# Interleaving the stages of neighbouring tiles on TensorE, with a ring of five x blocks and eleven weight slots

## The reference

```python
h = rmsnorm(x, norm_mix);  proj = h @ w_in            # 1024 -> 2048: u | gb | gc | v, 512 channels each
d = trailing_means(u, windows 2/4/8/16) - u           # along time, per group of 128 channels
a = (d @ w_pool[group]) * pool_scale
b = gb * causal_dwconv3(gc * v)
x = x + concat(a, b) @ w_out                          # 1024 -> 1024
h = rmsnorm(x, norm_ffn);  up = h @ w_up              # 1024 -> 5632
upc = causal_dwconv3(up) + bias;  val, gate = split(upc)
x = x + (silu(gate) * val) @ w_down                   # 2816 -> 1024
y = rmsnorm(x, norm_final)
```

## Time and profile before

| | |
|---|---|
| median of 3 runs | 826.86 us |
| the profiled execution | 826.7 us, its slowest core (1) spans 825.2 us |
| other cores | 806.0 to 824.5 us |
| mean granted TensorE clock, core 1 | 0.979 |
| PE busy | 722.6 us, 88% |
| DVE, ACT, POOL busy | 504.9, 358.9, 194.9 us |
| weight units | 120, of 512 KB as they land, 6.9 us from issue to landing |
| chain that ended last | PE 57%, DMA 14%, DVE 11%, ACT 8%, issue 7% |

### The profile page before, as it was taken

The page is one execution under the profiler, slowest core; times in us unless marked ns, Lnnn a source line. Parts: engine busy times, 40 slices in busy tenths (PEclk is TensorE's granted clock), DMA queues, the critical chain, the costliest instruction groups (busy, mean ns, idle before and its releaser), DMA issues.

```text
span 825.2 us, 12962 instructions; the slowest of 8 cores (806.0 to 825.2 us)
## 1 busy us (share of the span) xinstructions
PE 722.6 (88%) x3826; PEld 337.1 (41%) x3826; DVE 504.9 (61%) x878; ACT 358.9 (43%) x846; POOL 194.9 (24%) x381
## 2 busy tenths in 40 slices
PE   0296788889999998999999879999999898999996
PEld 0143344344445433444444334444444334444442
DVE  0446477668864466677753475677743576788822
ACT  1223337556662233365652333466642332666621
POOL 3022005444530010044420010144420010244300
PEclk9998899999999999999999999999999899999999
DMA  8959727976642198179962394199842591499421
GB/s 204 217 85 150 124 33 110 170 124 106 116 86 78 65 195 187 26 128 148 148 114 100 103 213 95 26 154 155 151 81 99 166 172 21 81 152 154 84 91 68
DMA packets 27751, 98.69 MB, mean 120 GB/s; under 512 B 3470, under 2 KB 3982, under 8 KB 27682
## 3 DMA queue, kind: packets, MB, share of 16 engines
q0 software_dynamic: 19584, 70.92, 51.9%
q1 hardware_dynamic: 8098, 26.95, 9.8%
HBM read 158.75 MB, written 10.01 MB: 205 GB/s over the span
## 4 chain that ended last, share of the span: by engine, by line
PE 57%; DMA 14%; DVE 11%; ACT 8%; issue 7%; SPq 1%; DVEq 0%; POOL 0%; ACTq 0%; POOLq 0%
PE G L446 39%; DMA wslot<-w_str 9%; PE G L660 8%; PE G L661 8%; DMA x<-xp 3%; ACT hbuf L387 3%; DMA xrot<-xp 2%; DVE x L669 1%; DVE x L668 1%; ACT arena L770 1%; PE TR L410 1%; ACT hb L387 1%; ACT rs_all L389 1%; PE G L686 1%; DVE hbuf L399 1%
## 5 line engine op out<-in xcount | busy, mean ns | idle before, releaser
L446 PE MATMUL G<-aT,wslot 128*128 128x512 bf16 x1408 | 311.8, 381 | 5.7 <-ACT Esave L795 2.3
L446 PEld LDWEIGHTS G<-aT,wslot 128*128 128x128 bf16 x1408 | 136.4, 98 | 172.1 <-issue 15.6
L770 ACT ACTIVATE arena<-G,cst_sb 128x512 f32<-128x512 f32 x176 | 134.3, 774 | 102.0 <-PE G L446 102.0
L779 DVE SCALAR_TENSOR_TENSOR arena<-G,cst_sb,arena 128x512 f32<-128x512 f32 x176 | 130.0, 748 | 58.6 <-ACT Esave L795 37.4
L446 PE MATMUL G<-hT,wslot 128*128 128x512 bf16 x512 | 121.6, 396 | 27.3 <-DVE hT L414 8.1
L364 POOL DMA_DIRECT2D wslot<-w_str x120 | 68.6, 572 | 322.4 <-PE G L446 286.3
L660 PE MATMUL G<-w_down_sb,actT 128*128 128x512 bf16 x352 | 133.4, 379 | 1.0 <-POOL actT L799 1.0
L661 PE MATMUL G<-w_down_sb,actT 128*128 128x512 bf16 x352 | 133.4, 379 | 0.0
L799 POOL TENSOR_TENSOR actT<-arena 128x512 bf16<-128x512 f32 x88 | 95.5, 1085 | 149.8 <-ACT arena L766 84.4
L788 DVE SCALAR_TENSOR_TENSOR arena<-G,cst_sb,arena 128x512 f32<-128x512 f32 x176 | 125.5, 744 | 4.9 <-DVE OFp L786 0.5
L387 ACT ACTIVATE hbuf<-x 128x1024 bf16<-128x1024 f32 x34 | 35.9, 1057 | 123.9 <-DVE x L669 119.0
(11 more groups left out here) (115 smaller groups left out, 585.8 us busy)
## 6 DMA issues: line engine op xcount, KB each, us to landing
wslot<-w_str POOLq DMA_DIRECT2D x120, 512.0 KB, 6.9
x<-xp SPq DMA_DIRECT2D x16, 512.0 KB, 13.6
yp<-x SPq DMA_DIRECT2D x16, 512.0 KB, 2.8
xrot<-xp SPq DMA_DIRECT2D x12, 512.0 KB, 12.5
w_down_sb<-w_down POOLq DMA_DIRECT2D x11, 512.0 KB, 13.0
w_out_sb<-w_out POOLq DMA_DIRECT2D x4, 512.0 KB, 20.3
stf_sb<-st_ffn SPq DMA_DIRECT2D x1, 704.0 KB, 9.8
o_ffn_s<-stf_sb SPq DMA_DIRECT2D x1, 704.0 KB, 3.7
```

Source lines behind the costliest of these rows:

```text
L446: ins = e.matmul(out_ap, lhsT=wslot[slot][:, k, half * 128:(half + 1) * 128], rhs=rhsT[:, k, 0:ncols], start=(k == 0), stop=(k == nk - 1))
L770: P.op("act", lambda e, tp=tp, g=g, c=c, h=h: e.activation(out=tp[:, h, 2:514], in_=G[g][:, :], func=AF.Identity, scale=cc(C_FW + 3 * c), ...
L779: P.op("dve", lambda e, tp=tp, g=g, c=c, h=h: e.scalar_tensor_tensor(out=tp[:, h, 1:513], in0=G[g][:, :], scalar=cc(C_FW + 3 * c + 1), in1 ...
```

## The change

- **Order on PE.** Behind stage 3 of tile s comes stage 1 of tile s+1 at once, then a new function `window`: blocks 0 to 2 of stage 4 of tile s, the four stage 2 blocks of tile s+1, and block 3 of stage 4 of tile s in three parts (k 0 to 8, 9 to 16, 17 to 21) with the last transposes of stage 2 between them. The stage 0 blocks of tile s+2 are woven into the stage 4 blocks; the fourth stands behind the first stage 2 block. Stage 0 of tile 1 is woven into stage 2 of tile 0.
- **x blocks.** `x1` becomes a ring of `NX` = 5 blocks. The block (s+1, i+1) is loaded by `load_x1` behind the store of block (s, i), into the place which that store frees.
- **Weights.** The small tile's buffers move into one area `sm_arena` of 8 blocks. Once they are dead (in the window of tile 0) seven of the blocks become weight slots 4 to 10, and the eighth the fifth x block. A unit is now issued when a slot is released (`release`, `pump`), and the w_down pieces are spread over the units up to the 30th.
- **Loads at the start.** SP loads the four x blocks first, then constants, small x and states; st_ffn and gfin wait for stage 1. POOL issues four weight units ahead of its constants. The first stage 1 pair runs block by block.
- **Smaller edits.** No warm matmuls. Stage 1's last pool matmuls (`laters`) run behind the first five k of two stage 2 blocks (tile 0), or behind the first stage 4 block. In tile 0 the small tile's stage 2 follows the four blocks, and its stage 3 matmuls run one step ahead. In stage 3 the history copy follows the two evictions.

```diff
 NW = 4
-DEBUG = False
-WARM_S2, WARM_S3A, WARM_S3B, WARM_S1 = 6, 12, 6, 6
+NX = 5
...
+        def xr_of(s, i):
+            return (4 * s + i) % NX
+
+        def load_x1(s, i):
+            r = xr_of(s, i)
+            r0 = (s * 4 + i) * 128
...
+            P.op("sp", lambda e: e.dma_start(out=x1[r], in_=xp[r0:r0 + 128, :]),
+                 writes=[("x1", r)] + extra, dsem=f"D_x1_{r}")
...
+        def norm1_block(s, i):
+            if s == 0:
+                src, sk = x1[i], ("x1", i)
+            else:
+                b = 4 * s + i
+                src, sk = xrot[b % 2][:], ("xrot", b % 2)
+                r0 = b * 128
+                P.op("sp", lambda e: e.dma_start(out=src, in_=xp[r0:r0 + 128, :]), writes=[sk], dsem=f"D_xrot{b % 2}")
+            hb, hk = next_hb()
+            return hb_done(hk, norm_transpose(src, 128, [sk], hb, hk, hT, i * 128, C_G1, [("hT", i)]))
...
+        def window(s, laters):
+            nx2 = s + 2 if s + 2 < NST else None
+
+            def n1(i):
+                return norm1_block(nx2, i) if nx2 is not None else (lambda: None)
+            load_x1(s + 1, 0)
+            pb = n1(0)
+            for i in range(3):
+                post = s4_block(s, i)
+                if i == 0:
+                    for fn in laters:
+                        fn()
+                pb()
+                post()
+                if i + 1 < 4:
+                    load_x1(s + 1, i + 1)
+                pb = n1(i + 1)
+            if s == 0:
+                s4_small()
+                free_slots.extend(range(NW, NW + 7))
+                pump()
+            n2 = []
             for i in range(4):
...
+                n2.append(s2_block(s + 1, i))
+                if i == 0:
                     pb()
...
+                if i >= 2:
+                    n2.pop(0)()
+            gab = (galloc(), galloc())
+            s4_mm(3, ALLK[0:9], True, False, gab)
+            n2.pop(0)()
+            s4_mm(3, ALLK[9:17], False, False, gab)
+            n2.pop(0)()
+            s4_mm(3, ALLK[17:NFF], False, True, gab)
+            return lambda: s4_post(s, 3, gab)
```

More of the change, by code:

```diff
@@ L207, in psum @@
             return es.enter_context(nc.psum_tensor(name, shape, dt))
-        wslot = [sb(f"wslot{i}", [128, 8, 256], BF16) for i in range(NW)]
+        wslot = [sb(f"wslot{i}", [128, 8, 256], BF16)[:] for i in range(NW)]
         w_out_sb = sb("w_out_sb", [128, 8, D], BF16)
@@ new lines, in build_nc, with pump @@
+        assert [i for k, i in plan if k == "r"] == list(range(len(resident)))
+        plan.reverse()
+        free_slots = list(range(NW))
+        slot_of = {}
+        alias_done = set()
+        def pump():
+            while plan:
+                kind, i = plan[-1]
+                if kind == "r":
+                    plan.pop()
+                    dst, src, key, name = resident[i]
+                    P.op("pool", lambda e, dst=dst, src=src: e.dma_start(out=dst, in_=src), writes=[key], dsem=name)
+                    continue
+                if not free_slots:
+                    return
+                plan.pop()
+                slot = free_slots.pop(0)
+                slot_of[i] = slot
+                extra = []
+                if slot >= NW and slot not in alias_done:
+                    alias_done.add(slot)
+                    extra = alias_keys[slot]
+                t = wplan[i]
+                P.op("pool", lambda e, slot=slot, t=t: e.dma_start(
+                    out=wslot[slot].rearrange("p a b -> p (a b)"), in_=w_str[t, :, :]),
+                    writes=[("W", slot)] + extra, dsem=f"D_w{slot}")
@@ new lines, in f, with s2_mm @@
+                for n, k in enumerate(ks):
+                    st, sp = first and n == 0, last and n == len(ks) - 1
+                    e.matmul(G[ga][0:nrows, :], lhsT=lhsT_of_k(k), rhs=wsb[:, k, 0:512], start=st, stop=sp)
+                    ins = e.matmul(G[gb][0:nrows, :], lhsT=lhsT_of_k(k), rhs=wsb[:, k, 512:1024], start=st, stop=sp)
+                return ins
+            P.op("pe", f, reads=[lkey_of_k(k) for k in ks] + list(wkeys), writes=[gk(ga), gk(gb), gt(ga), gt(gb)])
+        def s2_mm(i, ks, first, last, gab):
+            mm_part(lambda k: aT[:, k, i * 128:(i + 1) * 128], lambda k: ("aT", k, i), 128, w_out_sb, WOUT_KEYS,
+                    ks, first, last, *gab)
@@ L939, in build_nc @@
-        while res_i[0] < len(resident):
-            issue_resident(1)
+        pump()
+        mk_ident()
+        P.op("pool", mk_consts, writes=["epst", "invcnt", "zeros"])
+        load_states_s1()
+        pbs = []
+        for i in range(4):
+            pbs.append(norm1_block(0, i))
+            if i >= 1:
+                pbs.pop(0)()
+        pbs.pop(0)()
+        norm_transpose(xs_sb[0:NSM, :], NSM, ["xs"], hs, "hs", hTs, 0, C_G1, ["hTs"])()
+        laters = stage1(0)
+        load_states_s3()
@@ new lines, in build_nc @@
+        gabs = {}
+        for i in range(2):
+            gabs[i] = (galloc(), galloc())
+            s2_mm(i, S2_KORDER[0:5], True, False, gabs[i])
+        for fn in laters:
+            fn()
+        n2 = []
+        pb = norm1_block(1, 0)
+        for i in range(4):
+            if i < 2:
+                s2_mm(i, S2_KORDER[5:], False, True, gabs[i])
+                n2.append(s2_post(0, i, gabs[i]))
+            else:
+                n2.append(s2_block(0, i))
+            pb()
+            if i >= 1:
+                n2.pop(0)()
+            if i < 3:
+                pb = norm1_block(1, i + 1)
@@ new lines, in build_nc @@
+        sm2 = s2_small()
+        for fn in n2:
+            fn()
+        for s in range(NST):
+            last = (s == NST - 1)
+            if s == 0:
+                stage3(0, sm2)
+                sample_state_outputs()
+            else:
+                stage3(s)
+            if last:
+                prompt_state_outputs()
+                gabs = [(galloc(), galloc()) for _ in range(2)]
+                for i in range(2):
+                    s4_mm(i, ALLK[0:NFF - 1], True, False, gabs[i])
+                for i in range(2):
+                    s4_mm(i, ALLK[NFF - 1:], False, True, gabs[i])
+                    s4_post(s, i, gabs[i])
+                for i in range(2, 4):
+                    s4_block(s, i)()
+                continue
+            laters = stage1(s + 1)
+            post3 = window(s, laters)
+            post3()
```

400 lines of the change are left out of this document (184 added, 216 removed).

## The result

The changed kernel takes 878.73 us, the median of 4 runs (863.67 to 936.79), beside 826.14 us for the kernel before, measured with it. The ratio is 1.0496 [1.0444, 1.0548]: slower, where 820 was forecast. Profiled, it took 863.67 us. In every one of these executions two to eight of the cores had a mean granted clock of 0.925 or lower, beside about 0.95 on the others, and even the least disturbed ones, from which the ratio is taken, hold that loss. In the profiled one it is a stretch of 160 us at a granted clock of 0.81 on two cores. I compare stages on core 1, which has no such stretch.

What follows compares the result with a forecast made beforehand. PE was taken as busy nearly all the time in stages 2 to 4 of tiles 1 to 3, with losses in five places, the start first. The terms summed to -6.4 us, from 826.7 to 820.3, range 784 to 838.

Steps and rivals of the forecast that it cites:

- The windows: Stage 4 interleaved with the next tile's stage 2: +15.6 us in tile 0, +20.6 in tile 1, -12.8 in tile 2.
- The turn: Windows of tiles 0 and 1: stage 4 block's end through store, x and xrot loads and norm to PE's transposes, 17.9 us.
- late TR banks: Windows, behind the wait: DVE frees the two TR banks late, 5.3 us in tile 0, 0.8 in tile 1.
- no turn: Rival, windows: the loads do not hold PE, 769 us, or 795 with half of each wait; chance 0.15 for both.
- Slow turns: Rival, windows: the turn through the store takes longer, at 20.5 us the kernel takes 836; chance 0.2.
- Start: Kernel start: x and constants first in the queue, x landing at 17 us, first pair as if started at 21.1; -19.2 us.
- Stages 1 and 2 of tile 0: -2.2 us for matmuls put among the pool matmuls, +9.6 for stage 2 as a DVE chain of 7.8 us turns.
- 1.6 to begin: Stage 2 of tile 0: time ahead of four DVE turns (31.2 us), with 6.3 for the small tile, 39.1 in all.
- Stage 1 of the other tiles: Tile 1 takes 30.5 us (-1.9); tiles 2 and 3, with eleven slots, take 29.5 each (-6.7 and -3.8).
- Stage 3 of tile 0: w_down pieces no longer crowd its first steps; 22 steps less PE's lead at the end, 102.9 us, -5.6.
- The tail: Stages 3 and 4 of tile 3: no change predicted, 0 us.
- The clock: Rival: without filler the granted clock falls at six places, 3.0 us each, 18 in all, giving 838 us; chance 0.1.

Runs made afterwards that it cites:

- e1: Changed kernel with the xrot load of block i+1 issued ahead of the store of block i: 798.19 us, ratio 0.9622 to the kernel before.
- e15: Kernel before with only the start's loads reordered (constants, then tile 0's x blocks, small ones behind): 807.08 us, ratio 0.9818.
- e2: Changed kernel with constants loaded ahead of the x blocks and the small tile's transposes behind the first pair's matmuls: 844.35 us, ratio 1.0171.
- e5: Changed kernel with the copies out of TR between adds and reciprocal in stage 2 of tile 0: 861.53 us, two cores at low clock every time.
- e17: As e16, with the norms of tile 1 moved from stage 2 of tile 0 into its stage 3: 799.14 us, ratio 0.9647.
- e16: e13 with the small tile's stage 2 put back behind block 1 of stage 2 of tile 0: 789.58 us, ratio 0.9533.
- e13: Changed kernel with xrot loads two blocks ahead of the stores, plus the edits of e2 and e5: 786.71 us, ratio 0.9561.
- e9: Changed kernel with the sample states' stores moved from stage 3 of tile 0 to the end of stage 1 of tile 1: 858.51 us, ratio 1.0386.
- e4: Changed kernel with four weight slots to the end instead of eleven from the window of tile 0 on: 849.96 us, ratio 1.0234.
- e3: Changed kernel with 24 unread matmuls ahead of the transposes at each of the six waits for the norm: 845.38 us, ratio 1.0189.
- e6: Changed kernel unchanged, run again on another chip: 873.15 us (864.47 to 885.39).
- e11: Changed kernel unchanged, run once more on another chip: 846.82 us, ratio 1.0266.

## Why the prediction was wrong

**The windows: right in mechanism, and in size with some luck.** The turn was worked out as 17.9 us, and five of the six are 17.7 to 18.1. The waits came where they were forecast, and e1 shows the cause by taking them away. Their sizes in tile 1 were 7.73, 5.53 and 11.80 us, where 8, 8 and 14 had been worked out. The turn is the same, but behind a wait the granted clock is low (0.82 from 497.8 to 509.3 us, 0.70 from 515.9 to 520.9), so that PE's own part of a turn takes 12.6 and 6.0 us instead of 10.0 and 4.0. What the waits lost the matmuls took up, and the window came out 1.9 us below the sum. In tile 0 the first turn took 21.9 us, and the 5.3 us that were put down for late TR banks came out as 1.4 (0.75 and 0.60 us of idle time at the last transposes); the two errors and the low clock cancel to 0.6. The third window gained 12.7. The rival "no turn" did not occur. "Slow turns" occurred once in six: this xrot took 8.65 us to land, the one shown above 4.55, near the 5.43 of the earlier trace rows; the median of 12.5 of the earlier trace rows was not reached.

**The step that failed is the sum of what the change gives outside the windows:** -29.8 as predicted, -1.4 as measured. Its terms:

- *Start, -19.2, measured -10.2.* x landed as worked out: ACT takes its last block at 16.6 us. But the sum let x stand for everything. The constants are behind x in the queue and landed at 20.3, the small x at 24.4, and I let the small tile's transposes, which stand ahead of stage 1 in PE's order, count for nothing. e15 and e2 show both: with the constants first, the matmuls start at 22.2 and 24.6. The size of the prize was right (e15: 18 us). The term's own numbers, 17 + 5.2, also give a start at 22.2 and not the 21.1 that it uses.

```profile
16.58 1.06 ACT L449 ACTIVATE hbuf<-x1b 128x1024 bf16<-128x1024 f32 x1 [1.82 <-DMA x1b<-xp]
...
24.40 1.06 ACT L449 ACTIVATE sm_arena<-sm_arena 84x1024 bf16<-84x1024 f32 x1 [6.28 <-DMA sm_arena<-xsm]
```

- *Stages 1 and 2 of tile 0, +7.4, measured +12.0.* The chain on VectorE was not the loss: its turns are 7.2 us and less (7.8 predicted), and from the first residual add to stage 3 the changed kernel takes 33.4 us, where 4 x 7.8 + 6.3 = 37.5 had been worked out (22.4 in the kernel before). What failed is the part ahead of that add, "1.6 to begin" and the 2.2 taken off stage 1: from the second pair on it was to take 47.7 us instead of 55.2, and it took 56.2. PE's wait for the pooling stayed (6.97 us, 6.78 in the earlier trace rows), and at the handover from stage 1 to stage 2 it waits 1.25, 1.57, 0.89 and 0.89 us for results of VectorE and ACT, between 80.3 and 89.0 us. Of the surplus, e5 takes 3 to 5 us away by an order on VectorE, e17 another 3; e16 shows that the small tile's place is worth nothing. Of the 7.4 us by which stages 1 and 2 of e13 are longer than those of e15 (91.8 against 84.4), these runs leave some 4 unexplained. (Besides, 39.1 - 29.3 is 9.8, where the sum has 9.6.) The first residual add, the kernel before and the changed one:

```profile
100.96 0.69 DVE L668 TENSOR_TENSOR x<-G,x 128x512 f32<-128x512 f32 x1 [7.79 <-PE G L661]
...
91.82 0.69 DVE L745 TENSOR_TENSOR x1b<-G,x1b 128x512 f32<-128x512 f32 x1 [0.20 <-PE G L761]
```

- *Stage 1 of the other tiles, -12.4 in all, measured -1.1.* For tile 1 VectorE's backlog was named and given 2 us; it and the wslot waits are worth more, 6.0 us of waits for wslot in the changed kernel, and e9 shows that one hides behind the other. For tiles 2 and 3 I forecast 29.5 us each, from matmuls alone, and they are 31.5 to 32 in every variant, the slots full or not (e4): 1.05 us at arena and 1.51 at aT, waits for VectorE's chain of the pooling. The 4.1 us of waits for wslot that tile 2 had before did go, but with four slots as well, so the extra slots are not what removed them.
- *Stage 3 of tile 0, -5.6, measured -2.5.* The waits for weights went, as forecast, and waits for ACT's copy of the small tile's result (L879) came in their place: from the seventh step on one step takes 4.9 us instead of 4.82. The 3.1 us "less PE's lead at the end" stand in no row. PE's waits in this stage, the kernel before and the changed one:

```profile
PE G L446 <- DMA wslot<-w_str: 10.8, 6, 4.0
...
PE G L516 <- ACT sm_arena L879: 9.3, 16, 1.0
```

- *The tail, 0, measured +2.9:* stage 4 of tile 3 waits 3.31 us for the last actT, a wait that the kernel before does not have there. What makes it was not tested.

The start, the stages 1 and the tail have one fault in common: a handover between engines or queues (the small tile's transposes, the pooling chain, the last actT) was put at nothing. In stages 1 to 3 of tile 0 handovers were counted, but too short. Six such terms, all one way, are 31 us, and the stages 3 of tiles 1 and 2, which I gave nothing, returned 2.5. The range's upper end (838) had room for the rivals, not for these.

**The clock.** With the clock as the only loss, 838 was given. It is not the cause: e3 raises it in the windows and gains under 2 us. The Trainium skill, "TensorE: Matmul & The Clock Gate", section "HAM oscillation — how this bites in real kernels", has groups of matmuls start cold behind a wait for a DMA. The traces show this too (0.87 and 0.84 in the windows, 1.00 and 0.97 in e1), and that it costs little where a chain through other engines sets the time.

**The stretch at 0.81** was not foreseen, and adds 16 us to the slowest core of the profiled execution, the 43 us by which that execution missed being 27 + 16:

```profile
322.00:481.00 159.00, 157.01 (x620) 67.28 (x632) 98.09 (x144) 70.54 (x159) 41.46 (x53) 0.81 0.69 123
482.00:500.00 18.00, 17.89 (x89) 8.40 (x90) 7.21 (x11) 6.14 (x11) 0.53 (x1) 1.00 0.34 59
```

This is core 4 (columns as above): 0.81 from 322 to 481 us, 1.00 right behind it. Stage 3 of tile 1 takes 92.7 us on it and 76.4 on core 1. It is in the traces of the changed kernel, of e5 and of e6, and in none of the others, e11 with the same kernel among them. It need not belong to the change: in executions without a trace, pairs of cores fall in mean clock with other kernels too, the kernel before among them (cores 0 and 1 at 0.91, with 852.96 us where its others take 823 to 829). What sets it off is not shown.

## What to carry to other kernels

When a load moves behind a store on an in-order queue, write down the whole turn, from the end of the matmuls through store, load and norm back to PE, with durations from the trace: that gave 17.9 us and was right to about 1% in five turns of six, and one reordered issue was worth 48 us. Price a stage not by its busiest engine alone but with the waits that its trace already shows, and most of all what leads up to a chain's first link; a gain that is claimed for a buffer or a slot needs a wait on that buffer in the trace before. And test the cheap part by itself: the early x blocks alone gave 1.8% on the kernel before, and the interleaving gives more only once its loads are issued ahead (0.9561 in all).

## What the runs showed of the hardware

- A granted clock of 0.81, between the levels of 0.50 (1.2 GHz) and 1.00 (2.4 GHz), for 159 us on cores 4 and 5 at once, with cores 6 and 7 of the same die at 1.00; it began and ended between two matmuls with PE busy before and after it. In e6 all eight cores had such a stretch, on four of them for more than 220 us (lower still in places, behind waits).
- 104 KB of constants took 17.42 us to land behind 2 MB of x beside four weight units, and were at the head of the path; first in the queue they took 2.7 (e2) and no longer were.
- A store of 512 KB landed 2.82 us and the load behind it 4.55 us after issue in a window with a DMA share of 0.21, so that a turn through both is 8.4 us before any engine works; in the window of tile 0, at 0.46, one such load took 8.65.
